# ScalarE copies the transposed probabilities first and takes the newest exponential second

## The reference, cut to what matters

```
def nsa_attention(q, kv, gate_logits, rel_bias, cmp_k, cmp_v):
    ...
    def block(s0):
        ...
        s_s = (jnp.einsum('bqgjd,bgqkld->bgjqkl', qb, kb) * scale + bias_s).astype(jnp.float32)
        s_s = jnp.where(valid_s, s_s, NEG).reshape(b, g, hg, Q_BLOCK, SEL_TOPK * SEL_LEN)
        p_s = jax.nn.softmax(s_s, axis=-1)
        o_s = jnp.einsum('bgjqn,bgqnd->bqgjd', p_s, ...)
        ...
        p_w = jax.nn.softmax(jnp.where(valid_w, s_w, NEG), axis=-1)
        o_w = jnp.einsum('bgjqk,bkgd->bqgjd', p_w, vwb)
        return o_s, o_w
    ...
    o = gts[..., 0:1] * o_cmp + gts[..., 1:2] * o_sel + gts[..., 2:3] * o_win
```

## Time and profile before

| | |
|---|---|
| Median of 3 runs | 830.55 us (829.95 to 834.14) |
| The profiled execution's own time | 829.99 us |
| Its span, first to last instruction | 828.2 us |
| Mean granted TensorE clock | 0.993 |
| Busy over the span: PE, PEld, DVE, ACT, POOL | 96%, 78%, 52%, 40%, 34% |
| The chain of work that ended last | PE 86%, DVE 6%, ACT 4%, issue 3%, DMA 1% |

### The profile page before, as it was taken

One profiled execution on the slowest core, in us unless ns is written; L12 is line 12 of the kernel. 1 busy time (PEld: TensorE's weight loads), 2 busy tenths in 40 slices (PEclk: granted clock), 3 DMA queues, 4 the chain that ended last, 5 costly groups with the idle time before them and its releaser, 6 DMA issues.

```text
span 828.2 us, 11342 instructions
## 1 busy us (share of the span) xinstructions
PE 797.0 (96%) x4012; PEld 645.0 (78%) x4012; DVE 430.5 (52%) x778; ACT 328.6 (40%) x579; POOL 283.9 (34%) x123
## 2 busy tenths in 40 slices
PE   6999999999999989899999999999999999999995
PEld 4778988878766656568888888888888888888895
DVE  6554437775655566612437368772158314751254
ACT  6333223498856565563225333332122222222221
POOL 4242342511111111143434435444444444444430
PEclk9999999999999999989999999999999999999998
DMA  7832222210140000014313132222232222222213
GB/s 260 321 106 77 77 102 102 77 51 27 51 123 31 26 26 27 27 51 168 134 54 136 69 127 102 90 88 101 101 101 92 87 100 101 101 98 83 99 52 102
DMA packets 25477, 77.60 MB, mean 94 GB/s; under 512 B 3710, under 2 KB 6966, under 8 KB 25183
## 3 DMA queue, kind: packets, MB, share of 16 engines
q1 hardware_dynamic: 23612, 74.72, 26.2%
q10 hardware_dynamic: 1827, 2.37, 1.1%
HBM read 73.90 MB, written 2.13 MB: 92 GB/s over the span
## 4 chain that ended last, share of the span: by engine, by line
PE 86%; DVE 6%; ACT 4%; issue 3%; DMA 1%; SPq 0%; DVEq 0%; ACTq 0%
PE bank L1149 61%; PE bank L1415 2%; PE bank L1334 2%; PE bank L1397 2%; PE bank L1448 2%; PE bank L1452 2%; PE bank L1453 2%; DVE ns L1016 1%; PE bank L1169 1%; PE bank L1170 1%; PE bank L1171 1%; PE bank L1346 1%; ACT pt L677 1%; PE bank L1241 1%; PE bank L1376 1%
## 5 line engine op out<-in xcount | busy, mean ns | idle before, releaser
L467 POOL TENSOR_TENSOR wlo<-wraw,whi 128x1024 fp32r<-128x1024 f32 x117 | 281.2, 2408 | 508.5 <-ACT whi L500 262.6
L518 ACT ACTIVATE whi<-wraw 128x1024 fp32r<-128x1024 f32 x48 | 50.9, 1061 | 115.3 <-PE bank L1149 108.9
L500 ACT ACTIVATE whi<-wraw 128x1024 fp32r<-128x1024 f32 x63 | 66.0, 1053 | 45.7 <-PE bank L1149 23.1
L1149 PE MATMUL bank<-hh,wlo 128*128 128x512 f32 x304 | 82.8, 398 | 0.6 <-DVE gm L974 0.5
L1149 PE MATMUL bank<-hl,whi 128*128 128x512 f32 x304 | 82.2, 392 | 0.0
L1149 PE MATMUL bank<-hh,whi 128*128 128x512 f32 x304 | 80.9, 391 | 0.0
L1087 DVE TENSOR_TENSOR x_res<-bank,x_res 128x512 f32 (+1 forms) x28 | 19.4, 693 | 107.8 <-PE bank L1149 107.8
L1080 DVE TENSOR_TENSOR tmp<-tmp,rstd_b 128x512 f32<-128x512 f32 x32 | 67.2, 2101 | 1.1
L1149 PE MATMUL bank<-h2h,wlo 128*128 128x512 f32 x256 | 65.9, 391 | 0.0
L1149 PE MATMUL bank<-h2h,whi 128*128 128x512 f32 x256 | 65.5, 389 | 0.0
L1149 PE MATMUL bank<-h2l,whi 128*128 128x512 f32 x256 | 65.5, 389 | 0.0
(11 more groups left out here) (241 smaller groups left out, 1305.3 us busy)
## 6 DMA issues: line engine op xcount, KB each, us to landing
wraw<-in_panels SPq DMA_DIRECT2D x117, 512.0 KB, 3.3
w1k<-in_w SPq DMA_DIRECT2D x1, 2048.0 KB, 9.3
w1v<-in_w SPq DMA_DIRECT2D x1, 2048.0 KB, 13.8
hank<-bias_by_distance SPq DMA_DIRECT2D x4, 512.0 KB, 5.8
x_res<-in_xT SPq DMA_DIRECT2D x4, 512.0 KB, 4.3
out_dram<-x_res SPq DMA_DIRECT2D x16, 128.0 KB, 1.8
xs<-in_xT SPq DMA_DIRECT2D x4, 256.0 KB, 7.2
xs<-in_xT ACTq DMA_DIRECT2D x4, 256.0 KB, 6.6
```

Of the source, the lines that this page charges most:

```text
L467: nc.gpsimd.tensor_tensor(wlo[:, s], wraw[s][:], whi[:, s].bitcast(F32), ALU.subtract).then_inc(w_lo, 1)
L500: A(whi[:, s], wraw[s][:], ACT.Copy).then_inc(w_hi, 1)
L518: A(whi[:, s], wraw[s][:], ACT.Copy).then_inc(w_hi, 1)
L1149: ins = M(b[:, cols], lhs, (xl if a == 1 else xh)[:, row + k, cols], start=(m == 0), stop=(m == 23))
```

## The change

The block that copies the transposed probabilities of unit i - 3 moves to the front of ScalarE's step, ahead of the exponential of unit i and of the half-panel rounding. Nothing is added or removed, no wait is changed, and the other engines' lists stay as they are.

```diff
             for i in range(UNITS + 5):
                 if i == 2:
                     stick_out_high(PAIRS - 1)
+                u = i - 3
+                if 0 <= u < UNITS:
+                    r, run = unit(u)[3:]
+                    ps = result(act, ("t", u))
+                    if run >= 4 and run % 2 == 0 and r == 0:
+                        sparse_pv_done(act, run - 4)
+                    emptied(A(probs_tile(run, r),
+                              ps[:, 0:P * (r + 1)].rearrange("p (k t) -> p k t", k=r + 1), ACT.Copy), ("t", u))
                 if i < UNITS:
                     n = P * (unit(i)[3] + 1)
                     stored(act, ("s", i))
...
                 if i >= 9 and i % 10 in (9, 1) and i < UNITS:
                     split_half(P_GM + GM_SB + RING + (i - 9) // 10, i % 10 % 9)
-                u = i - 3
-                if 0 <= u < UNITS:
-                    r, run = unit(u)[3:]
-                    ps = result(act, ("t", u))
-                    if run >= 4 and run % 2 == 0 and r == 0:
-                        sparse_pv_done(act, run - 4)
-                    emptied(A(probs_tile(run, r),
-                              ps[:, 0:P * (r + 1)].rearrange("p (k t) -> p k t", k=r + 1), ACT.Copy), ("t", u))
```

## The result

The changed kernel takes 823.48 us (median of 7, 822.81 to 826.12), against 829.95 for the kernel before in the same comparison (7 runs). The ratio is 0.9925, 95% interval 0.9913 to 0.9937: 5.2 to 7.2 us faster. The profiled execution took 824.36 us, with a span of 822.6.

The account below looks back on a forecast made before the run. TensorE, busy 102.5 of 113 us in the sparse stage, idles mostly before turns, awaiting ScalarE's copy (7.7 us). Gains turn by turn summed to 4.6 us: 829.99 - 4.6 = 825.4, stated as a median of 825.8, range 822.8 to 829.0.

Parts of the forecast that it names:

- The copy's waits end: TensorE's turns in the sparse stage: all 14 waits for ScalarE's copy end, 7.7 us plus time not counted as idle.
- The scaling is late next: Turns then wait for VectorE's scaling of their own unit; these waits rise from 2.4 us to 4 or more.
- unit 33: Turn of unit 33 in the sparse stage: 1.18 us of idle time, of which 0.4 us is kept as gain.
- The exponential has cover: ScalarE's exponential, now behind the copy, costs 0 us (other bound 7.1), since VectorE does the next minimum first.
- L467 takes gains back: GpSimd's low part L467 stretches scalings beside it, leaving gains of only 0.3 and 0.1 us at units 20 and 30.
- units 20 and 30: Turns with waits of 1.08 and 0.72 us, caught by L467: 0.4 us gained together.
- the 18 waits that only the weight loads show: TensorE's turns: drains of about 0.1 us each, less what L467 takes back at units 41 and 51: 0.4 us.
- units 36 to 38: Turns of units 36 and 38, with waits of 0.55 and 0.61 us: 1.2 us gained together.
- the small ones: Four small waits before turns, 0.6 us in all, and their drains: 0.9 us gained.
- The rival in which it stays up at the end: Granted clock kept at the stage's end, last value product 2.38 instead of 4.54 us: 2.2 us more, 823.6; chance 0.15.
- The scaling rival: VectorE's scaling takes the copy's place before nearly every freed turn: some 2 us gained, 828.5; chance 0.25.
- The slower rival: 17 exponentials without a wait on ScalarE each delay the turn by a copy: +7.1 us, 832.9; chance 0.05.

Follow-up runs that it names:

- the experiment with a third bank: Kernel before, old ScalarE order, with turns rotating over three PSUM banks and scores over two: 825.28 us, ratio 0.9947.
- the profile with a full clock: Changed kernel run again with nothing edited: 824.37 us (4 runs); the profile is of its 820.54 us execution, without a stretch at 0.50.
- the copy in the middle: Kernel before, with the copy placed between the exponential and the half-panel rounding: 831.57 us, ratio 1.0019.
- filler at the end: Changed kernel, 24 gate matmuls moved from behind the stage into steps 64 to 67: 818.31 us; with half-panel roundings also moved beside value products: 812.25 us.

## Why the prediction was right, and where its sum was off

It said 825.8 us, range 822.8 to 829.0, and the time is 823.48. Direction and mechanism held, while the gain is larger than the 4.6 us of its sum (5.2 to 7.2 by the interval). Step by step:

- *The copy's waits end:* 7.7 us to none, and the experiment with a third bank shows that this claim makes most of the gain, 5.2 of the 6.6 us in the turns' times.
- *The scaling is late next:* 7.0 us in 10 waits, where 4 or more was said. Unit 38 gained what was worked out (0.77 said, 0.80 in the turns' times), unit 33 0.56 where 0.60 was the bound and 0.4 taken.
- *The exponential has cover:* VectorE waited 0.2 us, and even some 19 us of added work ahead of the exponentials cost nothing to be seen.
- *L467 takes gains back:* the gain of units 20 and 30 was put at 0.4 in all. In the profile with a full clock the turns gain 1.25 and 0.85 there and lose 0.91 and 0.79 right behind: 0.40.

The term that was mis-sized is the last of the sum, "the 18 waits that only the weight loads show ... less what L467 takes back": 0.4 said. Read from the turns' times of the profile with a full clock, the stage is shorter by 6.6 us up to the last turn instead of 4.6. By the terms of the sum: unit 33 0.56 (0.4 said), units 36 to 38 1.60 (1.2), units 52 and 53 0.95 (0.6), unit 17 0.54 (0.5), unit 2 0.05 net (0.2), the small ones 0.96 (0.9), units 20 and 30 0.40 (0.4), and the rest 6.58 - 5.06 = 1.5. That rest is a dozen turns that gain 0.07 to 0.27 each, and 0.05 at each turn behind a value product, less 0.38 and 0.24 at units 41 and 51. The sum had 18 drains of about 0.1 there and took 1.4 of the 1.8 back for L467 at units 41 and 51, where it took 0.62.

The other thing the sum lacked is the clock, in both directions. The rival in which it stays up at the end was right in its price (the value product falls from 4.54 to 2.38 us) and happens in some executions: the one of 820.54 is it. What I didn't foresee is the opposite, a stretch at 0.50 in the middle, which costs 1.65 us in some executions. With 6.6 us from the turns, the profile with the middle stretch has 4.9 of them left. That 825.8 was near owes something to this: turns that gained 2.0 us more than said and a clock stretch that took 1.65 of it back nearly cancel, which is luck. The sum also started from a median of 830.55 for the kernel before, and the comparison has 829.95.

The scaling rival, with 2 us of gain, had the right engine and the wrong size. The slower rival had no sign of it in any run.

## What to carry to other kernels

When an in-order engine serves two stations, put first the instruction whose input is already there and whose output another engine waits for; the one that must wait anyway then waits in nobody's way. Estimate the gain from what arrives next, turn by turn, and add up the small ones too: a dozen turns of 0.1 to 0.3 us made up a fifth of this gain. A wait that is removed shows the next one; here it was a GpSimd instruction beside a VectorE one, and moving its trigger by a few steps was worth nearly as much as the change.

## What the runs showed of the hardware

- A scaling that starts while GpSimd's subtraction runs ends with it (304.11 to 306.47 beside 303.95 to 306.32), one that starts 0.23 us ahead of it takes its usual 0.41 us. In all ten profiles each scaling that starts under L467 in this stage ends 0.08 to 0.29 us behind it. So whether 2 us are lost hangs on 0.4 us of order (0.16 behind the start of L467, or 0.23 ahead of it). The minimum is not held: with 512 columns it takes 0.69 us beside L467, and 0.68 to 0.69 without.
- The granted clock of the same kernel, with the same waits to 0.03 us, is 0.50 from 309 to 312 us in one execution and 1.00 in another. In the profile that shows it, TensorE was 13% busy in one microsecond at 305 and busy again for 2 us before the clock fell. The profiles of the third bank and of the copy in the middle have such a stretch too, behind waits of 1.28 and 1.45 us at unit 41; that of the kernel before, with 1.05 us there, has none. Every profile of a kernel with filler at the end has 1.00 through the whole stage, the one with the wait of unit 41 among them. Why that one keeps its clock in the middle, and whether it always does (4 executions, all at 0.996 or 0.997), stays open.
